# Late products in ten slots of twelve per chunk, two pairs of levels side by side, late loads issued by POOL

## The reference, cut to what matters

```python
proj = h @ w_in
(gq, gk, gv, g_low, gr, hq, hf, hi, hg, sz, sxbc, sdt, gates) = jnp.split(proj, offs, axis=-1)
...
# GLA and HGRN2, chunk by chunk, with per-channel decay b = cumsum(log_decay)
o_inter = einsum('bhcd,bhde->bhce', qi * exp(b), state)
scores = einsum('bhid,bhjd,bhijd->bhij', qi, ki, rel_decay)      # causal
state = state * exp(b_last)[..., None] + einsum('bhcd,bhce->bhde', k_to_end, vi)
# SSD, chunk by chunk
cb = einsum('bgin,bgjn->bgij', ci, bi)
y = einsum('bgrij,bgrjp->bgrip', decay * cb * dt, xi) + einsum('bgin,bgrpn->bgrip', ci, state) * exp(b)
...
g = sigmoid(gates)
merged = g[:, :, 0] * (y_gla @ w_br_gla) + g[:, :, 1] * (y_hgrn @ w_br_hgrn) + g[:, :, 2] * (y_ssm @ w_br_ssm)
```

## Time and profile before

| | |
|---|---|
| median of 3 runs | 2037.71 us |
| lowest and highest run | 2036.77, 2040.89 us |
| span of the profiled execution, first to last instruction | 2040.4 us |
| mean granted TensorE clock | 0.975 |
| PE busy, of the span | 94% |
| DVE, ACT, POOL busy | 72%, 51%, 11% |
| first late product to the last | 577.7 to 1085.6 us |

### The profile page before, as it was taken

One profiled execution on the slowest core, in us unless ns is written; L12 is line 12 of the kernel. 1 busy time (PEld: TensorE's weight loads), 2 busy tenths in 40 slices (PEclk: granted clock), 3 DMA queues, 4 the chain that ended last, 5 costly groups with the idle time before them and its releaser, 6 DMA issues. The chain is left out here.

```text
span 2040.4 us, 26797 instructions
## 1 busy us (share of the span) xinstructions
PE 1925.7 (94%) x10602; PEld 1576.7 (77%) x10603; DVE 1472.5 (72%) x1687; ACT 1048.0 (51%) x1234; POOL 218.3 (11%) x173
## 2 busy tenths in 40 slices
PE   6999999999999999999998999995999999999993
PEld 5789888888977777777776888874788888888881
DVE  5876467667227888788775656556889988999875
ACT  5234344444224545444444334223777887888763
POOL 3310000000030000000001000012122222222210
PEclk9999999999999999999998999997999999999996
DMA  5242332432355557656537654543999999999986
GB/s 168 86 145 73 114 104 97 131 104 93 107 145 158 151 160 168 167 127 152 160 115 282 206 204 182 229 178 138 349 376 384 389 386 385 389 386 387 387 331 259
DMA packets 212415, 436.11 MB, mean 214 GB/s; under 512 B 28018, under 2 KB 151042, under 8 KB 184770
## 3 DMA queue, kind: packets, MB, share of 16 engines
q1 hardware_dynamic: 179394, 355.68, 50.3%
q10 hardware_dynamic: 20864, 53.49, 7.5%
q0 software_dynamic: 12032, 25.22, 3.2%
HBM read 369.67 MB, written 81.43 MB: 221 GB/s over the span
## 5 line engine op out<-in xcount | busy, mean ns | idle before, releaser
L1602 PE MATMUL psum<-h_hi,l_hi 128*128 128x512 f32 x384 | 158.5, 413 | 4.9 <-PEq L58 3.3
L1602 PE MATMUL psum<-h_lo,l_hi 128*128 128x512 f32 x384 | 159.8, 416 | 0.0
L1602 PE MATMUL psum<-h_hi,l_lo 128*128 128x512 f32 x384 | 157.9, 411 | 0.0
L2741 DVE TENSOR_TENSOR gu_lo<-up_raw,gu_hi 128x2048 fp32r<-128x2048 f32 x64 | 146.3, 2288 | 13.2 <-ACT gu_hi L2684 13.2
L2684 ACT CAST gu_hi<-up_raw 128x2048 fp32r<-128x2048 f32 x64 | 122.1, 1909 | 35.0 <-PE u_ps L2813 35.0
L1258 ACT COPY l_out<-psum 128x512 f32<-128x512 f32 x48 | 28.1, 585 | 170.3 <-PE psum L1602 162.3
L2457 PE MATMUL mpsum<-y_hi,wb_hi 128*128 128x512 f32 x256 | 103.3, 403 | 10.1 <-DVE y_lo L2217 9.1
L2813 PE MATMUL g_ps<-gu_hi,xeT_hi 128*128 128x512 f32 x256 | 105.0, 410 | 5.8 <-DVE xeT_lo L2750 5.8
L806 DVE TENSOR_TENSOR w_lo<-w_raw,w_hi 128x512 fp32r<-128x512 f32 x90 | 61.9, 689 | 65.5 <-ACT w_hi L662 65.5
L662 ACT CAST w_hi<-w_raw 128x512 fp32r<-128x512 f32 x90 | 55.7, 622 | 91.9 <-PE ps L931 91.4
L2457 PE MATMUL mpsum<-y_lo,wb_hi 128*128 128x512 f32 x256 | 101.7, 397 | 0.0
(11 more groups left out here) (465 smaller groups left out, 5419.0 us busy)
## 6 DMA issues: line engine op xcount, KB each, us to landing
up_raw<-moe SPq DMA_DIRECT2D x62, 1024.0 KB, 8.1
gate_raw_a<-moe SPq DMA_DIRECT2D x33, 1024.0 KB, 8.4
gate_raw<-moe SPq DMA_DIRECT2D x33, 1024.0 KB, 8.4
dn_raw_a<-moe SPq DMA_DIRECT2D x31, 1024.0 KB, 7.2
dn_raw<-moe SPq DMA_DIRECT2D x31, 1024.0 KB, 8.0
w_raw<-w_in SPq DMA_DIRECT2D x26, 1024.0 KB, 6.1
l_raw<-w_gates ACTq DMA_DIRECT2D x24, 512.0 KB, 5.4
s_gates<-l_out ACTq DMA_DIRECT2D x48, 256.0 KB, 4.0
```

The costliest lines, as they stand in the source:

```text
L1602: ins = nc.tensor.matmul(psum[:, bank, :], w[t % 2][:, k, :], x[:, k, half * 512:half * 512 + 512], start=i == 0, stop=i == LATE_MM - 1, s ...
L2741: nc.vector.tensor_tensor(gu_lo[p][:], gu_raw[p][:], gu_hi[p][:].bitcast(F32), ALU.subtract).then_inc(gu_ready, 1)
```

## The change

On PE, SLOT becomes 12, and ten slots stand in a chunk for fifteen. Levels 0 and 1 stand side by side, and level 4 stands right ahead of the transposes of x. No slot stands behind the inter product any more, nor behind the means; the double slot behind level 6 is a single one. POOL issues the loads of the late tiles: two at its start, the others once DVE has made the low part of an earlier tile. ACT issues none. On ACT, the eviction of h0 + 1 stands ahead of the first eight differences, and relative 0 and 1 of the next chunk ahead of the squares of o. On DVE, the first two factor pairs of a chunk are made at the end of the chunk before, ahead of yt; two decs stand ahead of the diagonal's scores; cbm stands right behind factors 3, ahead of the sums of the chunk before; scores 4 stand ahead of a low part.

```diff
--- before.py
+++ after.py
@@ -1206,8 +1206,13 @@
 
         @block.gpsimd
         def _(pool):
+            def late_load(t):
+                pool.dma_start(l_raw[t % 2][:], io["w_gates"][t].rearrange("p (k n) -> p k n", k=KT)).then_inc(l_loaded[t % 2], 16)
+
             for b in range(2):
                 nc.gpsimd.memset(q_in[b][:, 0:4, :], 0.0).then_inc(q_zeroed, 1)
+            late_load(2)
+            late_load(3)
             nc.gpsimd.memset(ident[:], 0.0).then_inc(ident0, 1)
             pool.wait_ge(ident0, 1)
             nc.gpsimd.affine_select(out=ident[:], in_=ident[:], compare_op=ALU.not_equal, fill=1.0, base=0,
@@ -1234,16 +1239,13 @@
                                     pattern=[[1, CH]], channel_multiplier=-1).then_inc(const_ready, 1)
             nc.gpsimd.memset(mean_a[:], 1.0 / GLA_DV).then_inc(const_ready, 1)
             nc.gpsimd.memset(mean_b[:], 1.0 / 256).then_inc(const_ready, 1)
-
+            for t in range(4, LATE_T):
+                pool.wait_ge(l_split, t - 3)
+                late_load(t)
 
         @block.scalar
         def _(act):
             nc.scalar.preload_act_table_set(EXP_LN_SET)
-
-            def late_load(t):
-                if t >= 4:
-                    act.wait_ge(l_split, t - 3)
-                act.dma_start(l_raw[t % 2][:], io["w_gates"][t].rearrange("p (k n) -> p k n", k=KT)).then_inc(l_loaded[t % 2], 16)
 
             def late_hi(t):
                 act.wait_ge(l_loaded[t % 2], 16 * (t // 2))
@@ -1260,8 +1262,6 @@
                 act.dma_start(dr["gates"][h % 2, t % 8, :, t // 8, :], l_out[h % 2][:]).then_inc(l_stored[h % 2], 16)
                 if h % 2 and t + 2 < LATE_T:
                     late_hi(t + 2)
-                if h % 2 == 0 and h >= 2 and t + 3 < LATE_T:
-                    late_load(t + 3)
 
             def relative(c, lv):
                 i, h = NE * c + lv, LEVELS[lv]
@@ -1310,9 +1310,9 @@
                         nc.scalar.activation(wmat[:, h, :], wmat[:, h, :], ACT.Relu, scale=-1.0, bias=tok[:, c, 0, h:h + 1])\
                             .then_inc(seg_ready, 1)
 
+                late(h0 + 1)
                 act.wait_ge(small_ready, c + 1)
                 differences(range(SSM_HEADS // 2))
-                late(h0 + 1)
                 if c:
                     ssm_scale(c - 1)
                 relative(c, 6)
@@ -1331,17 +1331,15 @@
                 act.wait_ge(kT_ps_ready, c + 1)
                 nc.scalar.copy(flat(k_in[b][:]), mid_ps[:, 0:CT * P]).then_inc(kT_ready, 1)
                 late(h0 + 3)
+                if c < LAST:
+                    relative(c + 1, 0)
+                    relative(c + 1, 1)
                 act.wait_ge(o_ready, c + 1)
                 if c:
                     act.wait_ge(ya_stored, 16 * c)
                 nc.scalar.activation(flat(ya), o_ps, ACT.Square).then_inc(sq_ready, 1)
-                if c < LAST:
-                    relative(c + 1, 0)
-                    relative(c + 1, 1)
                 late(h0 + 4)
 
-            late_load(2)
-            late_load(3)
             project_stored(act)
             late(0)
             act.wait_ge(tok_ps_ready, 1)
@@ -1454,20 +1452,31 @@
                     ins = stt(yb[:, k, :], yt[:, k, :], nw_s[:, k:k + 1], rs2[:, k // 2, :], ALU.mult, ALU.mult)
                 ins.then_inc(yb_ready, 1)
 
+            def level_factors(c, lv):
+                b = c % 2
+                h, e = LEVELS[lv], ex[(NE * c + lv) % 3]
+                dve.wait_ge(e_ready, NE * c + lv + 1)
+                v = lambda x: x.rearrange("p (n w) -> p n w", w=2 * h)
+                k6 = v(flat(k_in[b][:]))
+                q8 = q_in[b][:].rearrange("p a (n w) -> p a n w", w=2 * h)
+                e6 = e[:].rearrange("p (a n w) -> p a n w", a=CT, w=2 * h)
+                ql = q_lv[lv % 2][:].rearrange("p (a n h) -> p a n h", a=QT, h=h)
+                tt(v(k_lv[lv % 2][:])[:, :, 0:h], k6[:, :, 0:h], v(e[:])[:, :, 0:h], ALU.mult)
+                tt(ql[:, 0:2], q8[:, 0:2, :, h:2 * h], e6[:, 0:2, :, h:2 * h], ALU.mult)
+                tt(ql[:, 2:8], q8[:, 2:8, :, h:2 * h], e6[:, :, :, h:2 * h], ALU.mult).then_inc(qk_ready, 1)
+
+            def first_factors(c):
+                if c == NCH:
+                    return
+                dve.wait_ge(qk_loaded[c % 2], 80 * turns(c))
+                level_factors(c, 0)
+                level_factors(c, 1)
+
             def body(c):
                 b, h0 = c % 2, PREFIX + PER_CHUNK * c
 
                 def factors(lv):
-                    h, e = LEVELS[lv], ex[(NE * c + lv) % 3]
-                    dve.wait_ge(e_ready, NE * c + lv + 1)
-                    v = lambda x: x.rearrange("p (n w) -> p n w", w=2 * h)
-                    k6 = v(flat(k_in[b][:]))
-                    q8 = q_in[b][:].rearrange("p a (n w) -> p a n w", w=2 * h)
-                    e6 = e[:].rearrange("p (a n w) -> p a n w", a=CT, w=2 * h)
-                    ql = q_lv[lv % 2][:].rearrange("p (a n h) -> p a n h", a=QT, h=h)
-                    tt(v(k_lv[lv % 2][:])[:, :, 0:h], k6[:, :, 0:h], v(e[:])[:, :, 0:h], ALU.mult)
-                    tt(ql[:, 0:2], q8[:, 0:2, :, h:2 * h], e6[:, 0:2, :, h:2 * h], ALU.mult)
-                    tt(ql[:, 2:8], q8[:, 2:8, :, h:2 * h], e6[:, :, :, h:2 * h], ALU.mult).then_inc(qk_ready, 1)
+                    level_factors(c, lv)
 
                 def diagonal_in(a):
                     n = NS * c + a
@@ -1486,16 +1495,13 @@
                     nc.vector.copy_predicated(score[:].rearrange("p (n w) -> p n w", w=2 * h)[:, :, h:2 * h],
                                               v(mask[lv][:]), v(sc_ps[lv % 2])).then_inc(score_ready, 1)
 
-                dve.wait_ge(qk_loaded[b], 80 * turns(c))
                 i0 = NE * c
-                factors(0)
-                factors(1)
+                dec(i0 + 3)
+                dec(i0 + 4)
                 if c:
                     dve.wait_ge(o_ready, c)
                 diagonal_in(0)
-                dec(i0 + 3)
                 diagonal_in(1)
-                dec(i0 + 4)
                 if c:
                     gla_hgrn_out(c - 1)
                 else:
@@ -1507,6 +1513,9 @@
                 scores_in(1)
                 dec(i0 + 5)
                 factors(3)
+                dve.wait_ge(cb_ready, c + 1)
+                tt(cbm[:], ssm_ps.rearrange("p (g t) -> p g t", t=CH), tri[:].unsqueeze(1).to_broadcast([P, SSM_GROUPS, CH]), ALU.mult)\
+                    .then_inc(cbm_ready, 1)
                 if c:
                     x_weighted(c - 1)
                     x_in_sum(c - 1)
@@ -1519,16 +1528,13 @@
                 dec(i0 + 6)
                 factors(4)
                 late(h0)
-                dve.wait_ge(cb_ready, c + 1)
-                tt(cbm[:], ssm_ps.rearrange("p (g t) -> p g t", t=CH), tri[:].unsqueeze(1).to_broadcast([P, SSM_GROUPS, CH]), ALU.mult)\
-                    .then_inc(cbm_ready, 1)
                 if c:
                     ssm_state(c - 1)
                 scores_in(3)
                 dec(i0 + 7)
                 factors(5)
+                scores_in(4)
                 late(h0 + 1)
-                scores_in(4)
                 factors(6)
                 dve.wait_ge(xT_ready, c + 1)
                 tt(xdt[:], mid_ps.rearrange("p (h e) -> p h e", e=SSM_HD),
@@ -1551,6 +1557,7 @@
                 dec(i0 + 9)
                 dec(i0 + 10)
                 late(h0 + 2)
+                first_factors(c + 1)
                 dve.wait_ge(small_ready, c + 1)
                 dve.wait_ge(inter_ready, c + 1)
                 if c:
@@ -1567,6 +1574,7 @@
             for i in range(3):
                 dec(i)
             late(1)
+            first_factors(0)
             for c in range(NCH):
                 if c == 1:
                     dve.wait_ge(par_in, 16 * N_PAR)
@@ -1604,7 +1612,7 @@
                     if i == LATE_MM - 1:
                         ins.then_inc(l_done, 1)
 
-            SLOT = LATE_MM // 3
+            SLOT = LATE_MM // 2
 
             def heads():
                 for h in range(GLA_HEADS):
@@ -1677,7 +1685,6 @@
                     intra(c - 1, 1)
                 fill(SLOT)
                 level(c, 0)
-                fill(SLOT)
                 level(c, 1)
                 fill(SLOT)
                 level(c, 2)
@@ -1713,7 +1719,7 @@
                 level(c, 5)
                 fill(SLOT)
                 level(c, 6)
-                fill(2 * SLOT)
+                fill(SLOT)
                 pe.wait_ge(qk_ready, NE * c + NE)
                 pe.wait_ge(xdt_ready, c + 1)
                 for a in range(CT):
```

## The result

The changed kernel takes 2051.64 us (median of 4 runs, 2050.71 to 2053.58) against 2037.43 before (median of 4 runs, three of them those of the table above): a ratio of 1.0072, interval 1.0059 to 1.0086. It is slower by 14 us, where 16 us less were forecast.

What follows compares the result with a forecast made beforehand. PE was taken as the bound, busy 55.2 of 58 us in one chunk. The terms -29.2 - 5.8 + 13.6 + 4.8 + 0.4 = -16.2 us took 2037.7 to 2021.5, range 2014 to 2028 (chance 0.60).

Steps and rivals of the forecast that it cites:

- Late loads off ACT, squares and cbm earlier: In the chunks, PE's waits ahead of the means and transposes of B go, with their clock falls: -29.2 us.
- The price of a fall: At the four matmuls of the means, each fall of PE's clock was taken to lose 2.1 us.
- rival A: PE's clock falls at new waits, slot 9 (2038, chance 0.08) or slot 7 in odd chunks too (2046.7, 0.05).
- Slots, fewer runs: On PE, four fewer runs of late products in each of eight chunks save entering and leaving: -5.8 us.
- Slot 9: Behind the transposes of k, PE waits for ACT's copy and eviction, 1.7 us late in eight chunks: +13.6 us.
- Slot 7: Behind level 5, PE waits for the eviction of h0+2, 1.1 us in odd chunks, 0.1 in even: +4.8 us.
- PE is the later everywhere: DVE's and ACT's new order has its results ready before PE wants them throughout the chunk: 0 us.
- rival B: DVE binds: b landing from 22 on makes level 4 late, 1 to 2 us in seven chunks; 2028.5 to 2035.5, chance 0.16.
- Rival D: The old waits for squares and cbm stay, something other than the late load holding the squares: 2050.7 us, chance 0.03.

Runs made afterwards that it cites:

- e7: Changed kernel with the fifteen old slots, and on ACT the first eight differences ahead of the eviction of h0+1 as before: 2023.95 us.
- e1: Changed kernel with v's load issued behind the loads of x and z instead of ahead of b's load for all heads: 2034.31 us.
- e9: Changed kernel with the late loads on ACT's queue again, behind the eviction of each odd half: 2055.98 us.
- e4: Kernel before with PE's program of the change alone, ten slots of twelve; ACT, DVE and loads as before: 2061.53 us.
- e5: Changed kernel, v's load behind x and z; ACT evicts h0+3 ahead of the copy of k, h0+2 ahead of the last two exponentials: 2021.91 us.

## Why the prediction was wrong, step by step

- **Late loads off ACT, squares and cbm earlier: -29.2.** Right as to place, near in size. Neither L1665 nor L1708 waits after; in chunk 5 the squares start right at the end of the gate (914.50 plus 1.23, to 915.76) and end 1.9 ahead of the means. What the two places cost before, from start to start over chunks 1 to 7, was 27.3: the waits, and five falls at 1.5 to 1.6.
- **The price of a fall: 2.1.** This step took a row of another place. The 1.31 of the earlier trace rows is the means behind chunk 7 with a late product next; in the chunks the transposes of B come next, and at full clock the four products then take 1.82, as in chunk 7 of the kernel before:

```profile
1030.38 1.98 PE L1657 MATMUL psum<-y_out,mean_b 128*128 128x512 f32 x4 [2.41 <-ACT y_out L1283]
1032.20 0.60 PE L1701 MATMUL psum<-ident_m,bc_in 128*128 128x128 f32 x4
```

  Against 3.41 with the fall that is 1.6, not 2.1. The five falls were 8, not 10.5; rival A's time at eight falls would be 2034 and not 2038.
- **Slots, fewer runs: -5.8.** Near. A chunk of the kernel before without what PE waits is 54.0 (e7, with the same slots, has 53.99 in chunks 2 and 6). Chunk 4 of the changed kernel, 58.28, is 53.4 without its three waits (2.31, 0.83 and 1.71 from start to start), where 53.0 was forecast. That is 0.6 a chunk, some 4.8 in all. The ten slots are shorter by 1.1 to 1.3 a chunk, but products that no slot follows now take longer to the next start: the means of the norm 1.81 for 1.31, the product with the state 1.88 for 1.71.
- **Slot 9: +13.6.** Right to 0.01 us: 1.71 a chunk.
- **Slot 7: +4.8.** Right in size. After, it is 1.15 to 1.17 idle in chunks 1, 3 and 7, 0.78 in chunk 4 and 0.23 in chunk 5; in e1 0.60 to 0.78 in chunks 1 to 7.
- **"PE is the later everywhere: 0", and rival B.** Here it failed. I took b's load at its old 16.0 us from its issue and put its landing near 18; it took 18.0 to 21.4, since it shares the DMA engines with a burst of which eb and v had moved 2.8 us closer. The argument against rival B, that the load starts where it did behind the same instruction, was true (2.1) and no argument. And I looked for its harm at level 4, with a cover of 3.7 us and a point of decision at 22. The first that stands behind it is ACT: wd, two exponentials and the one of eb (1.4 us), then the eviction that slot 5 wants. The point is 19.8, a cover of 1.8 us behind a landing at 18. The prediction did not follow wd on to ACT. Level 4 never waited for it, slot 5 did, and with its falls that is 19.1 of the 22.9 us below.
- **The sum, on the profile.** The diagonals of chunks 1 and 7 are 354.7 apart; the forecast's chunks (55.8 and 54.8) give 331.8. Of the 22.9 between, the delays of slot 5 are 13.3 from start to start, the three falls behind them 5.8 (1.5, 1.5 and 2.8), two short waits ahead of the transposes of x 1.3; the remaining 2.5, 0.4 a chunk, is work above the 53.0.
- **Rival A.** Clock falls came, three, none behind the waits of 1.47 at slot 9 or of 1.17 and less, all behind waits of 2.7 to 3.4. The rule of the Trainium skill quoted there (TensorE: Matmul & The Clock Gate, HAM oscillation), whose example on the page has longer waits than the 1.7 us weighed here, did not strike at slot 9.
- **Rival D.** Its time, 2050.7, is within 1 us of the measured one, and that is chance: the old waits, which it kept, are gone.

The time itself moved 14 us, and the profiled stage 6.2, once the clock behind its first product is left out. Some of the rest is the four runs of before: against the three later medians of the kernel before (51 runs, 2033 to 2049) the changed kernel is 12 to 13 us slower. Where the other 6 us are is open. Falls of the clock outside the chunks, like the one near 89, may be part of it; no profile of a second execution of either kernel shows how many a usual run has.

## What to carry to other kernels

A load's duration is not a property of the load: before moving work across the point that issues a group of transfers, measure from the first issue of the group to the last landing, and move that whole length against the first instruction, on any engine, that stands behind it. Then look at in-order engines between: here a transfer for DVE held an eviction on ACT that had nothing to do with it. And a stream of accumulating products through a single PSUM bank needs, at each end of a tile, other work at least as long as what the evicting engine has in front of its eviction; where the tiles end matters more than how often PE changes between kinds of work.

## What the hardware showed that I had not expected

- 512 KB loads took 3.6 us alone and 10 to 22 us inside the burst, on POOL's queue (up to 18.8) and on ACT's (up to 21.9).
- The issue alone of such a load took ACT's queue 3.4 to 7.3 us at the end of a chunk (e9, e4), and in the longest ACT stood idle for 6.3 us.
- The same load of b took from 14.8 to 23.2 us by what else was under way.
- PE's clock fell to 1.2 GHz behind waits of 1.9 us and more (e9: 1.91 and 1.99), but not behind each: in e5 two of three waits of 2.1 to 2.3 had a fall, in e1 one of 2.3 had none. Behind the forty waits of 1.47 at slot 9 in five kernels none was seen. A fall cost 1.5 to 1.6 us, 2.4 to 2.8 where the half clock lasted longer.
